# Decoder trunk on one core: gate and up products with the high and low part of the input side by side

## The reference

```python
def swiglu(x, wg, wu, wd):
    return (jax.nn.silu(x @ wg) * (x @ wu)) @ wd

for l in range(DEPTH):
    g = norm_g[l]
    h = rmsnorm(x, g[0])
    x = x + 0.5 * rmsnorm(swiglu(h, ffn_w_gate[l, 0], ffn_w_up[l, 0], ffn_w_down[l, 0]), g[1])
    ...
    h = rmsnorm(x, g[6])
    x = x + 0.5 * rmsnorm(swiglu(h, ffn_w_gate[l, 1], ffn_w_up[l, 1], ffn_w_down[l, 1]), g[7])
```

## Time and profile before

| | |
|---|---|
| Median of 3 runs | 1205.79 us (1201.29 to 1206.11) |
| The profiled execution, its time | 1199.31 us |
| The profiled execution, its span | 1197.6 us |
| Mean granted TensorE clock | 0.983 of full |
| PE / PEld busy | 1121.3 us (94%) / 1034.6 us (86%) |
| DVE / ACT / POOL busy | 669.6 us (56%) / 564.4 us (47%) / 72.7 us (6%) |
| DMA | 193.08 MB, 161 GB/s in the mean |

### The profile page before, as it was taken

How to read it: one execution, slowest core, us unless ns; L and a number is a source line. 1 busy time by engine, 2 the same in 40 slices (tenths; PEclk the granted TensorE clock), 3 DMA queues, 4 the chain that set the end, 5 groups by cost and what they waited for, 6 DMA issues and landing times.

```text
span 1197.6 us, 18619 instructions
## 1 busy us (share of the span) xinstructions
PE 1121.3 (94%) x7634; PEld 1034.6 (86%) x7634; DVE 669.6 (56%) x829; ACT 564.4 (47%) x798; POOL 72.7 (6%) x168
## 2 busy tenths in 40 slices
PE   6999999999879999999999999999978888999997
PEld 6999999997758899999989999988847777999997
DVE  5655545743876665454475554556664655555553
ACT  6544434635637664334364443435354555443341
POOL 4000000100011010000020000002000102000000
PEclk9999999999989999999999999999989898999999
DMA  8566564533333546655536656654142343556551
GB/s 268 157 205 202 175 186 165 171 99 124 106 106 124 176 159 212 208 168 186 176 113 222 212 176 185 201 159 144 44 151 102 120 136 111 198 177 209 177 176 69
DMA packets 144348, 193.08 MB, mean 161 GB/s; under 512 B 3270, under 2 KB 127116, under 8 KB 144284
## 3 DMA queue, kind: packets, MB, share of 16 engines
q1 hardware_dynamic: 143020, 187.93, 48.5%
q0 software_dynamic: 1264, 4.25, 1.0%
HBM read 191.12 MB, written 1.05 MB: 160 GB/s over the span
## 4 chain that ended last, share of the span: by engine, by line
PE 81%; DVE 8%; ACT 5%; DMA 2%; issue 2%; POOL 2%; SPq 0%; POOLq 0%; DVEq 0%; ACTq 0%
PE psum L768 20%; PE psum L671 15%; PE psum L673 15%; PE psum L672 15%; PE psum L930 4%; PE psum L755 3%; PE psum L682 2%; PE psum L683 2%; PE psum L684 2%; DVE w_lo L1755 2%; ACT w_hi L1194 1%; PE psum L818 1%; DVE x_state L1797 1%; ACT w_hi L1190 1%; DVE w_lo L1750 1%
## 5 line engine op out<-in xcount | busy, mean ns | idle before, releaser
L671 PE MATMUL psum<-h_hi,w_hi 128*128 128x256 f32 x1568 | 447.3, 285 | 7.6 <-DVE w_lo L1755 6.0
L1755 DVE TENSOR_TENSOR w_lo<-raw,w_hi 128x2048 fp32r<-128x2048 f32 x162 | 370.8, 2289 | 144.0 <-ACT w_hi L1194 143.7
L672 PE MATMUL psum<-h_lo,w_hi 128*128 128x256 f32 x1568 | 445.9, 284 | 0.0
L673 PE MATMUL psum<-h_hi,w_lo 128*128 128x256 f32 x1568 | 445.8, 284 | 0.0
L1194 ACT ACTIVATE w_hi<-raw 128x2048 fp32r<-128x2048 f32 x162 | 310.2, 1915 | 225.5 <-DMA raw<-in_ffn_w_gate 127.0
L671 PEld LDWEIGHTS psum<-h_hi,w_hi 128*128 128x128 f32 x1568 | 303.2, 193 | 10.1 <-DVE w_lo L1755 6.4
L672 PEld LDWEIGHTS psum<-h_lo,w_hi 128*128 128x128 f32 x1568 | 303.2, 193 | 1.7 <-issue 0.2
L673 PEld LDWEIGHTS psum<-h_hi,w_lo 128*128 128x128 f32 x1568 | 303.1, 193 | 0.0
L768 PE MATMUL psum<-w_hi,g_both 128*128 128x512 f32 x640 | 178.4, 390 | 0.7 <-DVE g_both L1861 0.7
L768 PEld LDWEIGHTS psum<-w_hi,g_both 128*128 128x128 f32 x640 | 117.6, 188 | 23.3 <-DVE g_both L1861 0.9
L1848 DVE TENSOR_TENSOR work<-psum,lat 128x512 f32<-128x512 f32 x44 | 30.4, 691 | 148.5 <-PE psum L673 143.3
(11 more groups left out here) (256 smaller groups left out, 1258.6 us busy)
## 6 DMA issues: line engine op xcount, KB each, us to landing
raw<-in_ffn_w_gate SPq DMA_DIRECT2D x44, 1024.0 KB, 5.3
raw<-in_ffn_w_up SPq DMA_DIRECT2D x44, 1024.0 KB, 5.3
raw<-in_ffn_w_down SPq DMA_DIRECT2D x44, 1024.0 KB, 5.0
raw<-in_ab_w_in SPq DMA_DIRECT2D x9, 1024.0 KB, 5.4
gain_row<-in_norm_g POOLq DMA_DIRECT2D x8, 512.0 KB, 6.0
raw<-in_xa_wk SPq DMA_DIRECT2D x4, 1024.0 KB, 5.3
raw<-in_ab_w_out SPq DMA_DIRECT2D x4, 1024.0 KB, 4.9
raw<-in_xa_wq SPq DMA_DIRECT2D x4, 1024.0 KB, 5.4
```

The source lines that it names most:

```text
L671: nc.tensor.matmul(o, wh, a_hi[:, k, :], start=(k == 0), stop=False)
L672: nc.tensor.matmul(o, wh, a_lo[:, k, :], start=False, stop=False)
L673: last = nc.tensor.matmul(o, wl, a_hi[:, k, :], start=False, stop=(k == KT - 1))
L1755: nc.vector.tensor_tensor(w_lo[:, c % RING, 0:k * n], raw[:, c % RAWS, 0:k * n], w_hi[:, c % RING, 0:k * n].bitcast(F32), ALU.subtract).th ...
```

## The change

The high and the low part of the input now lie side by side in one buffer `h_both`, 512 columns for each slice k. In the gate and up products the high part of the weights meets both in one matmul of 512 columns: the first 256 columns of the bank hold high by high, the last 256 high by low. The product with the low part of the weights stays 256 wide and is added to the first 256 columns. A half chunk so fills a whole bank of its own, and its two halves have to be added: DVE does this with a `tensor_reduce` over pairs of columns 256 apart, into `gs` or into a new buffer `up_sum`. A pair needs four banks (names Ga, Gb, Ua, Ub) where it needed two, and a bank is free when it has been summed. The scale and the product with silu then read SBUF. For pair 0 the sums of G stand right behind `row_scale`.

```diff
     def ffn(s):
         fill(s)
-        out.extend(f"{w}{s}.{p}" for p in range(PAIRS) for w in "GU")
+        out.extend(f"{w}{s}.{p}{j}" for p in range(PAIRS) for w in "GU" for j in "ab")
...
-        h_hi = sb("h_hi", [P, KT, TOK], F32R)
-        h_lo = sb("h_lo", [P, KT, TOK], F32R)
+        h_both = sb("h_both", [P, KT, 2, TOK], F32R)
+        h_hi, h_lo = h_both[:, :, 0, :], h_both[:, :, 1, :]
...
+        up_sum = work[:, 1024:2048].rearrange("p (a n) -> p a n", a=2)
...
-                s, p = map(int, name[1:].split("."))
-                v = FFNS[s] * PAIRS + p + 1
-                freed[name] = (scaled_done if name[0] == "G" else gu_done, v)
+                s, p = map(int, name[1:-1].split("."))
+                freed[name] = (sum_done, 4 * (FFNS[s] * PAIRS + p) + SUMS.index(name[0] + name[-1]) + 1)
...
+            def gate_or_up(name, i=0, gate=None):
+
+                hi, lo = weights(C[name], i)
+                for j in range(2):
+                    out_ = take(f"{name}{'ab'[j]}", i)
+                    o = slice(P * j, P * (j + 1))
+                    for k in range(KT):
+                        if gate is not None and j == 0 and k % 4 == 0:
+                            for t in range(NT):
+                                input_ready(gate, t, k // 4)
+                        if k:
+                            nc.tensor.matmul(out_[:, 0:TOK], lo[:, k, o], h_hi[:, k, :], start=False, stop=False)
+                        last = nc.tensor.matmul(out_[:, :], hi[:, k, o], h_both[:, k].rearrange("p a n -> p (a n)"),
+                                                start=(k == 0), stop=(k == KT - 1))
+                        if k == 0:
+                            nc.tensor.matmul(out_[:, 0:TOK], lo[:, k, o], h_hi[:, k, :], start=False, stop=False)
+                    filled(f"{name}{'ab'[j]}", last)
...
                 def triple(p, i=0):
-                    feature_major(f"G{s}.{p + 1}", h_hi, h_lo, i=i)
+                    gate_or_up(f"G{s}.{p + 1}", i)
                     if p == 0:
                         row_factors()
-                    feature_major(f"U{s}.{p + 1}", h_hi, h_lo, i=i)
+                    gate_or_up(f"U{s}.{p + 1}", i)
...
+                def sums(w, p, dst, i=0):
+                    for j in range(2):
+                        name = f"{w}{s}.{p}{'ab'[j]}"
+                        dve.wait_ge(*later(full(name), 4 * TURN // BANKS, i))
+                        nc.vector.tensor_reduce(dst[:, p % 2, TOK * j:TOK * (j + 1)],
+                                                bank(name).rearrange("p (a n) -> p n a", a=2), AX.X, ALU.add)\
+                            .then_inc(sum_done, 1)
+                    dve.wait_ge(sum_done, freed[name][1] + 4 * TURN * i)
+
                 def gate_scale(p, i=0):
-                    dve.wait_ge(*later(full(f"G{s}.{p}"), 2 * TURN // BANKS, i))
-                    nc.vector.tensor_tensor(gs[:, p % 2, :].rearrange("p (a n) -> p a n", a=2),
-                                            bank(f"G{s}.{p}").rearrange("p (a n) -> p a n", a=2),
-                                            rbc.unsqueeze(1).to_broadcast([P, 2, TOK]), ALU.mult)\
+                    if p:
+                        sums("G", p, gs, i)
+                    g = gs[:, p % 2, :].rearrange("p (a n) -> p a n", a=2)
+                    nc.vector.tensor_tensor(g, g, rbc.unsqueeze(1).to_broadcast([P, 2, TOK]), ALU.mult)\
                         .then_inc(scaled_done, 1)
 
                 def gate_up(p, i=0):
+                    sums("U", p, up_sum, i)
                     dve.wait_ge(silu_done, base + p + 1 + TURN * i)
-                    dve.wait_ge(*later(full(f"U{s}.{p}"), 2 * TURN // BANKS, i))
-                    nc.vector.tensor_tensor(gu[:, p % 2, :], sg[:, p % 2, :], bank(f"U{s}.{p}"), ALU.mult)\
+                    nc.vector.tensor_tensor(gu[:, p % 2, :], sg[:, p % 2, :], up_sum[:, p % 2, :], ALU.mult)\
                         .then_inc(gu_done, 1)
...
                 split_to(c0 + 2)
                 row_scale(s)
+                sums("G", 0, gs)
                 split_to(c0 + 3)
                 if s == 0:
                     mem_lo()
                 split_to(c0 + 4)
                 dve.wait_ge(rbc_done, FFNS[s] + 1)
```

More of the change, by code:

```diff
@@ L355, in build @@
         bank_read = [sem(f"bank_read{i}") for i in range(BANKS)]
+        sum_done = sem("sum_done")
         scaled_done, silu_done, gu_done = sem("scaled_done"), sem("silu_done"), sem("gu_done")
@@ L397, in build @@
         TURNS = (PAIRS - PEEL - 2) // TURN
-        assert PEEL + TURN * TURNS + 2 == PAIRS and 2 * TURN % BANKS == 0
+        assert PEEL + TURN * TURNS + 2 == PAIRS and 4 * TURN % BANKS == 0
         assert 3 * TURN % RING == 0 and 3 * TURN % RAWS == 0
+        SUMS = ("Ga", "Gb", "Ua", "Ub")
         freed, count = {}, [0] * BANKS
@@ L436, in used @@
                 return down_done, n_down[c]
-            return full(LAST_USE.get(name, name))
+            return full(name + "b" if name[0] in "GU" else LAST_USE.get(name, name))
         def bank(name):
@@ L640, in take @@
                     s, v = freed[tickets[n - BANKS]]
-                    pe.wait_ge(s, v + TURN * i)
+                    pe.wait_ge(s, v + 4 * TURN * i)
                 return psum[:, 4 + n % BANKS, :]
@@ L862, in ffn @@
                 begin(s)
-                feature_major(f"G{s}.0", h_hi, h_lo, gate=s)
-                feature_major(f"U{s}.0", h_hi, h_lo)
+                gate_or_up(f"G{s}.0", gate=s)
+                gate_or_up(f"U{s}.0")
                 if s == 0:
@@ L873, in ffn @@
                     for w in "GU":
-                        assert next(order) == f"{w}{s}.{p}"
+                        for j in "ab":
+                            assert next(order) == f"{w}{s}.{p}{j}"
                 p = PAIRS - 1
-                feature_major(f"G{s}.{p}", h_hi, h_lo)
-                feature_major(f"U{s}.{p}", h_hi, h_lo)
+                gate_or_up(f"G{s}.{p}")
+                gate_or_up(f"U{s}.{p}")
                 pair = [(C[f"D{s}.{q}"], g_hi[:, q % 2], g_lo[:, q % 2]) for q in (p - 1, p)]
@@ L1185, in hi_half @@
                     s, v = used(c - RING)
-                    act.wait_ge(s, v + (0 if s is down_done else 2 * TURN // BANKS) * i)
+                    act.wait_ge(s, v + (0 if s is down_done else 4 * TURN // BANKS) * i)
                 if name[:2] in ("xk", "xv"):
```

## The result

| | kernel before | changed kernel |
|---|---|---|
| median of the runs | 1204.67 us (20 runs, 1201.29 to 1207.01) | 1209.22 us (20 runs, 1205.47 to 1213.05) |
| profiled execution, span | 1199.31, 1197.6 us | 1207.01, 1205.2 us |
| mean granted clock | 0.983 | 0.974 |

The change makes the kernel slower: the ratio is 1.004 with an interval of 1.0029 to 1.005, that is 4.6 us. I had forecast 1204.8 us, 1.0 us faster than before. The time is inside the range, and the answer "within 0.5%" holds, but the direction was wrong. The two profiled executions are 7.7 us apart and their spans 7.6 us.

A forecast was written before the change was run, and what follows sets the result against it. TensorE was taken as the bound, busy throughout the FFNs. Terms -17.6 + 4.2 + 6.6 + 1.6 + 4.2 = -1.0 us gave 1204.8 us, with an 8-in-10 range of 1196.5 to 1213 us.

The forecast's parts named there:

- within 0.5%: Whole kernel: the time stays too close to the kernel before to tell from no change, 6 us; chance 0.62.
- wide product: TensorE's gate and up chunks: each of 1408 steps falls from 0.360 to 0.3475 us, saving 17.6 us.
- start of FFN 0, without the clock: FFN 0: G(1) and U(1) wait for banks that VectorE sums late, costing 4.2 us.
- starts of FFNs 3, 4 and 7: U(1) waits for the sum of U(0) behind the scaled G(0): 2.2 us each, 6.6 us for three.
- the four ends: Before D(10) in each FFN, the last half's sum lengthens the chain: 0.4 us each, 1.6 us in all.
- clock: Holds at FFN starts make the granted clock fall two or three times, 1.7 us each, 4.2 us in sum.
- The holds at the starts: TensorE idles before U(1) in FFNs 3, 4 and 7, about 2.2 us each, and before G(1) and U(1) in FFN 0.
- The sums: VectorE: each added reduction of 512 PSUM elements into 256 takes 0.69 us, hidden in the loop with 4.9 us left.
- The three rivals on the slower side: Narrow product hides nothing, +12 to +17 us (0.07); slow sums make VectorE the bound (0.10); TensorE not the loop's bound, +17 (0.03).

The follow-up runs named there:

- The run with the end alone: Changed kernel, with ScalarE splitting D(10) before instead of after the silu of the last pair in each FFN; 1203.41 us, ratio 0.9994 to the kernel before.
- the kernel with the edit that gives nothing: Kernel before, without the wide product, with only ScalarE's split of D(10) moved ahead of the last silu; 1203.83 us against 1203.34, ratio 1.0.
- the three executions with these starts: Changed kernel (1209.22 us), it with ScalarE's D(10) split before the last silu (1203.41), and it with all matmuls 256 wide again (1222.72).

## Why the prediction was wrong

By the spans (7.6 us between them):

| term | forecast | measured |
|---|---|---|
| wide product | -17.6 | -15.5 |
| start of FFN 0, without the clock | +4.2 | +4.4 |
| starts of FFNs 3, 4 and 7 | +6.6 | +6.7 |
| the four ends | +1.6 | +5.8 |
| clock | +4.2 | +6.0 |
| sum | -1.0 | +7.4 |

By the start times of the same matmuls the four FFNs alone are 7.8 us longer: behind D(10) each loses another 0.13 us, which the table leaves out. That everything else comes to -0.2 us is luck, a balance between two executions: G(0) starts 0.4 us later, a fall of the clock at 395 us, which before has not, costs 1.2 us, and the fall at 611 us that before had the earlier trace rows did not come, 1.6 us.

(FFN 0: D(0) comes 35.62 us after G(0) instead of 29.07, 6.55 later, and the 0.7 of the four shorter chunks are lost in it. G(1) there took 34.17 to 42.63, 8.46 us, where 5.6 is its time at 2.4 GHz, so 2.9 of these 7.3 us belong to the clock and 4.4 to the holds.)

- **The step that failed is the end of each FFN**, priced at 0.4 us and measured at 1.44, 4.2 us in all and the largest error of the sum. I wrote that the sum of the last half goes in front of the chain and adds 0.72 us "with its wait". I had followed VectorE's order from D(9) on and taken the row before it, the split of D(10), as done, since it ended 0.07 us before D(9). But the sums of G(10) also delay the silu, and ScalarE's part of that split stands behind the silu. ScalarE began the silu at 602.14, 3.95 us before D(9); before it was 4.83 us. The split moved by that 0.9 us to 0.8 us after D(9), and both sums of U(10) went behind it. The product after them (L1886) starts 2.05 us behind D(9), not 0.27; 0.34 us of that was slack, and 1.44 us is the hold. The run with the end alone takes the split out of the path and leaves 0.32 us, which I had forecast as 0.4.
- **The wide product was mis-sized.** 0.350 us for a step, not 0.3475: 32 steps take 16.63 - 5.44 = 11.19 us. The overhead that goes with the removed matmul is 13 ns in the rows, and 10 came back in the steps, since the wide products there are 0.230 us apart and not 0.2275. The down chunk gave 0.02 to 0.03 us for a turn that nobody forecast. Over 44 turns the two leave 15.5 us of 17.6, 2.1 us short.
- **The clock was mis-sized**, as far as one pair of executions tells. Three falls, in the two or three places that I expected, but the one in FFN 0 cost 2.9 us and not 1.7: G(1) ran at 1.2 GHz from its first matmul. Part of the 6.0 us is chance: the kernel with the edit that gives nothing shows, without any new hold, a fall in U(1) of FFN 0 at 46 us.
- **The holds at the starts were right** in mechanism and size: 2.24 us against 2.2 (442.8 - 440.56, the prediction's own figures, are nearer to 2.3), released by a sum, and gone when the sums move.
- **The sums were right:** 0.687 us, hidden in the loop. The Trainium skill, page "VectorE: DVE Perf Modes", section "Rules for kernel authors", calls tensor_reduce VectorE's slowest operation; here it took what an elementwise pass over 512 PSUM elements takes (0.691 us).

End, product and clock together took the sum from -1.0 to +7.4 us. Of that the medians show +4.6, because before's profiled execution was one of its quickest. The granted clocks point at the clock for the 3 us: the profiled executions have 0.983 and 0.974, but the mean over 17 executions of before is 0.977 and over the 20 of the changed kernel 0.973. Lost clock (one less the granted part, times the span) so differs by 4.7 us in the mean and by 11 us between the two profiled executions; an upper bound, since idle time at the lower clock costs nothing. That the time fell inside the range rests on its width: the forecast change had the wrong sign. The three rivals on the slower side were wrong as mechanisms: the wide product did hide an overhead, VectorE was not the bound, and in the loop the bound was TensorE. The kernel became slower in another way, by small holds that added up, which I had in the sum at too small a size.

## What to carry to other kernels

When a change gives an engine more to do, follow its order backwards from the wait as well as forwards. An operation that used to end 0.07 us before it was needed has no slack, and what delays the engine that feeds it decides. When an eviction frees a buffer, place it where the buffer is full, not where its value is used: the same sums cost 4.6 us net in one order and left 13.6 us of gain in another. And a saving spread over 44 turns in hundredths of a microsecond is no match for a handful of holds, so count both before trusting the sum.

## What the hardware showed that was not expected

- The same idle time of 1.89 us lowered the clock twice and left it alone once, with the same work before and after it; over the three executions with these starts (idle times of 1.89 to 1.98 us) it fell in FFN 7 three times, in FFN 3 twice and in FFN 4 never. A fall cost 1.55 us there and 2.9 us behind 3.67 us of idle time. The four waits of 1.30 us at the ends changed nothing.
- A 512-wide matmul on this path had two spacings in a steady stream: 0.227 us (down chunk) and 0.230 us (gate and up).
- A reduction of 512 PSUM elements into 256 pairs that lie 256 columns apart takes 0.687 us, as one into 2 elements does.
